# A modulation step moved one projection unit later, with other fetch places, in a fused hybrid attention layer

## What is computed

```python
mod = einsum('bd,de->be', silu(c), w_ada) + b_ada
shift, scale, gate = split(mod, 3, axis=-1)
h = rmsnorm(x, ln_gain) * (1 + scale[:, None]) + shift[:, None]
proj = einsum('btd,de->bte', h, w_in)
q_a, ckv, krope, g_a, q_b, k_b, v_b, q_i, k_i, w_i, g_b = split(proj, ...)
...   # latent attention (group A), sparse top-k attention (group B)
y = concat([rmsnorm(o_a, out_gain_a) * silu(g_a), rmsnorm(o_b, out_gain_b) * silu(g_b)])
out = x + gate[:, None] * (y @ w_out)      # and a last rmsnorm
```

## Time and profile before

| | us |
|---|---|
| median of three runs | 912.44 |
| lowest and highest of them | 912.41, 913.57 |
| the profiled execution | 913.76 |
| its span, from first to last instruction | 912.0 |
| TensorE busy in the span | 882.1 (97%) |
| VectorE, ScalarE busy | 414.2 (45%), 322.9 (35%) |

### The profile page before, as it was taken

One profiled execution on the slowest core, in us unless ns is written; L12 is line 12 of the kernel. 1 busy time (PEld: TensorE's weight loads), 2 busy tenths in 40 slices (PEclk: granted clock), 3 DMA queues, 4 the chain that ended last, 5 costly groups with the idle time before them and its releaser, 6 DMA issues.

```text
span 912.0 us, 13675 instructions
## 1 busy us (share of the span) xinstructions
PE 882.1 (97%) x5533; PEld 767.9 (84%) x5533; DVE 414.2 (45%) x851; ACT 322.9 (35%) x600; POOL 119.2 (13%) x191
## 2 busy tenths in 40 slices
PE   3899999999999999999999999999999999999996
PEld 1376788999999688888999998999999999888886
DVE  3522443335422144443333268464455566677362
ACT  3222343433421243322322254332334345554252
POOL 1000003101200000102120301000122223530000
PEclk9899999999999999999999999999999999999999
DMA  8999956475443222557553377755698843793413
GB/s 341 408 408 409 406 200 222 149 258 175 142 125 111 71 91 86 164 156 243 166 160 107 117 247 255 268 186 180 232 322 282 263 146 110 274 300 122 136 57 129
DMA packets 53599, 187.43 MB, mean 206 GB/s; under 512 B 7872, under 2 KB 8568, under 8 KB 52384
## 3 DMA queue, kind: packets, MB, share of 16 engines
q1 hardware_dynamic: 39488, 141.32, 43.7%
q0 software_dynamic: 13904, 44.71, 15.4%
q10 hardware_dynamic: 144, 0.52, 0.1%
HBM read 175.93 MB, written 12.69 MB: 207 GB/s over the span
## 4 chain that ended last, share of the span: by engine, by line
PE 84%; DVE 3%; ACT 2%; issue 1%; ACTq 0%; DVEq 0%
PE proj L1821 34%; PE proj L1810 28%; PE proj L1840 2%; PE proj L1791 2%; PE bankO L1919 2%; PE bankO L1928 2%; PE bankS L1840 1%; PE bankS L1982 1%; DVE w_lo L1302 1%; PE bankO L2001 1%; PE bankO L2000 1%; PE bankO L2009 1%; PE bankO L1969 1%; PE bankS L1810 1%; PE bankS L2025 1%
## 5 line engine op out<-in xcount | busy, mean ns | idle before, releaser
L1302 DVE TENSOR_TENSOR w_lo<-raw,w_hi 128x1024 fp32r<-128x1024 f32 (+2 forms) x164 | 196.8, 1205 | 227.5 <-ACT w_hi L979 226.6
L979 ACT ACTIVATE w_hi<-raw 128x1024 fp32r<-128x1024 f32 (+2 forms) x164 | 167.6, 1026 | 204.5 <-PE proj L1810 102.7
L1821 PE MATMUL proj<-hT_hi,w_hi 128*128 128x384 f32 x608 | 210.9, 347 | 0.0
L1821 PE MATMUL proj<-hT_hi,w_lo 128*128 128x384 f32 x608 | 203.8, 335 | 0.0
L1821 PE MATMUL proj<-hT_lo,w_hi 128*128 128x384 f32 x608 | 203.4, 335 | 0.0
L1810 PE MATMUL proj<-w_hi,hT_hi 128*128 128x512 f32 (+2 forms) x464 | 178.8, 385 | 1.8 <-DVE w_lo L1302 1.5
L1810 PE MATMUL proj<-w_hi,hT_lo 128*128 128x512 f32 (+2 forms) x464 | 174.3, 376 | 0.0
L1810 PE MATMUL proj<-w_lo,hT_hi 128*128 128x512 f32 (+2 forms) x464 | 174.1, 375 | 0.0
L1821 PEld LDWEIGHTS proj<-hT_hi,w_hi 128*128 128x128 f32 x608 | 114.2, 188 | 9.5 <-issue 7.8
L1821 PEld LDWEIGHTS proj<-hT_lo,w_hi 128*128 128x128 f32 x608 | 114.3, 188 | 0.5 <-issue 0.2
L1821 PEld LDWEIGHTS proj<-hT_hi,w_lo 128*128 128x128 f32 x608 | 114.1, 188 | 0.0
(11 more groups left out here) (372 smaller groups left out, 1044.3 us busy)
## 6 DMA issues: line engine op xcount, KB each, us to landing
raw<-in_units SPq DMA_DIRECT2D x184, 512.0 KB, 3.8
araw<-in_units SPq DMA_DIRECT2D x64, 512.0 KB, 8.8
kcT<-in_dsa_k_t POOLq DMA_DIRECT2D x8, 512.0 KB, 6.5
vc<-in_cache_dsa_v POOLq DMA_DIRECT2D x8, 512.0 KB, 5.8
gate_scratch<-stage POOLq DMA_DIRECT2D x8, 384.0 KB, 3.4
raw<-in_units SPq DMA_DIRECT2D x8, 336.0 KB, 4.4
raw<-in_units SPq DMA_DIRECT2D x8, 320.0 KB, 5.1
x_sb<-in_x_prompt SPq DMA_DIRECT2D x2, 1024.0 KB, 6.6
```

Source lines behind the costliest of these rows:

```text
L979: return nc.scalar.activation(out, in_, func, scale=scale, **kw)
L1302: V.tensor_tensor(w_lo[:, SLOT[u], 0:w], raw_of(u)[:, 0:w], high(u)[:, 0:w].bitcast(F32), ALU.subtract).then_inc(lo_ready, 1)
L1821: ins = mm(banks[blk][:, 0:TOK], w[:, n, cols], a[:, kt, :], start=first and n == m == 0, stop=final and n == per - 1 and m == 2)
```

## The change

The order of a quarter becomes: four ada units, a kb0 unit, five ada, a ga0 unit, seven ada, a ga1 unit, then `modT`, then a kb0 unit. The steps `modT`, `h` and `hl` of quarters 1 to 3 are put at the ga1 unit, one unit after the quarter's last ada unit. The projection units are fetched 4, 3, 2 or 0 places ahead instead of 6. From the ga1 unit of quarters 1 and 2 on, one unit more is split than LEAD would give. VectorE's step `rk` waits for the store of ga1 instead of ga0. Steps that are placed from the end of ada3 (`ld_const`, `bias` and others) come one unit earlier, since ada3 now ends one unit earlier.

```diff
-        out += ada[:4] + [keys[2 * q - 2]] + ada[4:8] + [first[q - 1]] + ada[8:12] + [keys[2 * q - 1]] + ada[12:]
-        out.append(second[q - 1])
+        out += ada[:4] + [keys[2 * q - 2]] + ada[4:9] + [first[q - 1]] + ada[9:] + [second[q - 1], keys[2 * q - 1]]
...
-AHEAD = 6
+AHEAD = {(CHUNK_OF["kb", 0], 2 * q): 4 for q in range(4)}
+AHEAD.update({(CHUNK_OF["ga", 1], q): 2 for q in range(4)})
+AHEAD.update({(CHUNK_OF["kb", 0], 2 * q + 1): 0 for q in range(4)})
...
-    for u in [u for u in order if CHUNKS[UNITS[u][0]][0] != "ada" and u < last + 3]:
+    for u in [u for u in order if CHUNKS[UNITS[u][0]][0] != "ada" and u < last + 2]:
...
-        order.insert(max(first, at - AHEAD), u)
+        order.insert(max(first, at - AHEAD.get(UNITS[u], LEAD)), u)
...
     if u < FIRST_UNIT["ckv", 0]:
-        return near
+        turns = [LAST_UNIT["ada", q] + 1 for q in (1, 2)]
+        return max([near] + [sum(v <= w + 6 for v in SPLIT_UNITS) for w in turns if w <= u])
...
-        u = LAST_UNIT["ada", q]
+        u = LAST_UNIT["ada", q] + (q > 0)
...
-            stored(dve, "ga", 0)
+            stored(dve, "ga", 1)
```

More of the change, by code:

```diff
@@ L156, in halved @@
         return 0
-    near = sum(v <= u + LEAD for v in SPLIT_UNITS)
+    done, near = sum(v <= u for v in SPLIT_UNITS), sum(v <= u + LEAD for v in SPLIT_UNITS)
     if u < FIRST_UNIT["ckv", 0]:
-        return near
-    return min(max(near, sum(v <= u for v in SPLIT_UNITS) + LEAD - 1), SPLIT_OF[W3_UNITS[LEAD - 1]])
+        turns = [LAST_UNIT["ada", q] + 1 for q in (1, 2)]
+        return max([near] + [sum(v <= w + 6 for v in SPLIT_UNITS) for w in turns if w <= u])
+    return min(max(near, done + LEAD - 1), SPLIT_OF[W3_UNITS[LEAD - 1]])
 def splits(u):
```

## The result

| | before | after |
|---|---|---|
| median of 19 runs each, us | 913.05 | 914.60 |
| lowest and highest | 912.37, 914.52 | 913.14, 916.91 |
| ratio of after to before, 95% interval | | 1.0015 (1.0009 to 1.0021) |
| the profiled execution | 913.76 | 913.14 |
| its span | 912.0 | 911.4 |

The changed kernel is slower by 1.5 us. I had forecast 911.2 us, faster by 1.2 us. The two profiled executions point the other way round, and this has to be known before one reads them: the profile of before is an execution above its median, and the profile of after is the fastest of its 19. A second profile of after is among the experiments.

The account below looks back on a forecast made before the run. DMA and TensorE were taken as both full. Idle of 2.98 us leaves and 2.9 comes; 0.2 us of the first block and about 0.35 a quarter remain: 1.25 us gained, put on the median, 911.2 us, range 909.9 to 912.4.

Parts of the forecast that it names:

- The ring: Ada buffers in quarters 1 to 3: fetches get 4.0 to 4.2 us to land; no gap taken, 3.8 us at 5.4 each.
- Rival 3: Ada buffers run dry in quarters 1 to 3, delaying place 77 by 3.8 us: 915.0 us, slower; chance 0.12.
- rival 4: Granted clock falls at a quarter's end; one fall in quarter 3 costs 5.1 us: 916.3 us; chance 0.08.
- The median: Whole kernel: the 1.25 us shift, 912.5 us for the profiled execution, was put on the median of before: 911.2 us.
- Rival 2: No gain: the new order ends on a landing, whatever time the clock lost before it: 912.4 us; chance 0.15.
- The cadence: Fetched units up to place 77 land every 1.283 us without a break, kb0.7 near 114.2 us.
- The removed waits: TensorE's waits for `modA` (quarters 1 to 3) and for `w_lo` at kb0.2 and kb0.4 go: 2.98 us.
- the new ones: TensorE waits 0.5, 0.8, 0.8 us before ada1.15, ada2.15, ada3.15 and 0.8 us for `hT_lo` at kb0.6: 2.9 us.
- The split of kb0.7 ahead of `modT`: End of quarter 3: its `w_lo` delays VectorE, so TensorE waits 0.8 us for `hT_lo`; kb0.6 starts at 120.4 us.
- No dip of the clock: Sign: the forecast is wrong if the granted clock dips after 50 us.
- The term for fewer ada groups: Each quarter gains about 0.35 us: one ada group fewer to switch to, and tails of matmuls before the waits.
- rival 1: New waits don't form since units land earlier than expected: 4.2 us gained, 908.2 us; chance 0.10.

Follow-up runs that it names:

- twelve buffers: The changed kernel with twelve instead of eight buffers for ada units, in use from quarter 1 on: 912.54 us, ratio 0.9992.
- before, ring of 12: The kernel before with twelve instead of eight ada buffers, orders as before: 913.51 us, ratio 1.0002.
- the same, last split late: The changed kernel with twelve ada buffers, and kb0.7 split behind the modulation of quarter 3 instead of ahead of it: 911.64 us, ratio 0.9983.
- before with the early splits: The kernel before, with kb0.2 and kb0.4 split before the modulation of quarters 1 and 2, order unchanged: 912.47 us, ratio 0.9991.
- before, ring of 6: The kernel before with six instead of eight ada buffers, all orders as before: 915.34 us, ratio 1.0028.
- after without the early splits: The changed kernel with kb0.2 and kb0.4 split behind the modulation again: 915.69 us.
- after, old fetch places: The changed kernel with every projection unit fetched 6 places ahead again, eight ada buffers: 918.56 us, ratio 1.0054.
- The halved ada units: Both kernels with half of each ada unit not fetched, the first half multiplied twice (wrong results): old order 911.99 us, new order 908.80 us.

## Why the prediction was wrong

The forecast of 911.2 us missed by 3.4 us, and the runs split this in two.

**The ring, 2.1 us: the failed step.** The prediction said: "I take no gap, since the nearer row is the unsaturated one: a fetch that would leave a gap meets an idle queue." With twelve buffers, where the gap does not arise, the same order takes 912.54 us, not 914.60. The trace counts sixteen arrivals for each fetch, and I read each as one of the sixteen DMA engines being through with its share (the times are worked out from the trace; no view lists them, and they don't name the engine). In the first trace of after:

| | issued | first arrival | last arrival |
|---|---|---|---|
| ada1.11 | 42.17 | 50.55 | 52.71 |
| ada1.12 | 49.58 | 52.68 | 53.98 |

By this reading the engines are 2.2 us apart. When ada1.12 is issued the fastest has 1.0 us of work left, and its next share arrives 3.1 us after the issue: 2.13 us from arrival to arrival instead of 1.28, 0.85 lost. The slowest has 3.1 us left and loses nothing. So the rate falls to 260 GB/s and the landing at 53.98 is still in time. What is lost is the lead of the fast engines: the distance shrinks from 2.2 to 1.3 us. A later delay of single engines, which that lead would have hidden, now makes the unit late. In the first trace of after kb0.2 (place 36) lands 0.36 us late in that way; in the second a unit at place 60 lands 1.3 us late, its other arrivals within 0.2 us of their time. In the trace of after with twelve buffers the engines stay 2.4 us apart from place 25 to the end, and no unit is late, though three arrivals at place 38 are 0.3 to 0.5 us late. At kb0.7 the first arrival is at 112.26 us before and 112.04 with twelve buffers, and at 113.50 and 114.14 in the two traces of after: there the fast engines have lost 1.5 and 2.1 us. Such delays of single engines stand in all traces; what makes them was not tried.

I had priced the ring as if one fetch landed late at each quarter and the queue were whole again after it. The shortest fetch of `araw` after 45 us sorts the traces:

| kernel | shortest, us | kb0.7 landed, us | median, us |
|---|---|---|---|
| before, ring of 12 | 12.6 | 113.97 | 913.51 |
| after, ring of 12 | 10.4 | 114.42 | 912.54 |
| the same, last split late | 10.4 | 113.92 | 911.64 |
| before with the early splits | 6.5 | 113.96 | 912.47 |
| before, two traces | 5.4, 6.6 | 114.18, 114.29 | 913.05 |
| after, two traces | 4.4, 4.2 | 114.97, 116.54 | 914.60 |
| before, ring of 6 | 4.0 | 116.68 | 915.34 |
| after without the early splits | 3.7 | 118.19 | 915.69 |
| after, old fetch places | 3.3 | 120.18 | 918.56 |

From 5.4 us on the last landing lies within 0.5 us of 114.2; at 4.4 and less it is late, and the later the shorter (of the 116.54 us in the second trace of after, 1.3 are the single engine). I had the bound of 5.4 us in the earlier trace rows, the only row of the saturated stretch, and took the 3.8 us of the earlier trace rows instead, a median over the whole kernel. Rival 3 had the right mechanism, and it got 0.12. That its 915.0 us is close to 914.60 is luck: its delay of 3.8 us measured 2.1, and the 911.2 us that it is added to measured 912.54. Two of the sums around it were slightly off: the gain is eaten from 4.55 us on (0.55 + 0.35 + 0.35 = 1.25) and not from 4.8, and rival 4 with the half of rival 3 makes 0.14 and not 0.15.

**The median, 1.3 us.** From the layout I had 912.5 us for the profiled execution, and then wrote "I put the shift on the median", 911.2 us. That median was of three executions, 912.44; of 19 it is 913.05, which is 0.6 of the 1.3 us. Rival 2 contradicts that step in the same text: the new order ends on a landing, whatever happened before. The order with twelve buffers bears rival 2 out: 912.54 us, with kb0.6 at 120.46, and hardly any spread. A shift read in one execution may be put on the median only if the time lost before it, here at the clock, is still lost in the new order.

**What held.** The cadence: kb0.7 lands between 113.96 and 114.42 us in every trace with a shortest fetch of 5.4 us or more (forecast 114.2). The removed waits, the new ones and their places. The split of kb0.7 ahead of `modT` in quarter 3: its wait was 0.52 us, forecast 0.8, and removing its cause, with twelve buffers, gained 0.9 us in the median. No dip of the clock between 50 and 900 us in the two traces of after.

**The term for fewer ada groups was right, and its counterpart was left out.** I gave each quarter 0.35 us for one ada group fewer and for tails of matmuls before the removed waits. The halved ada units show it without a wait for DMA. kb0.2 and kb0.4 start there, in the old order and in the new one, at:

```profile
68.52 0.50 PE L1810 MATMUL proj<-w_hi,hT_hi 128*128 128x512 f32 x1 [0.76 <-DVE w_lo L1302]
...
94.92 0.50 PE L1810 MATMUL proj<-w_hi,hT_hi 128*128 128x512 f32 x1 [0.73 <-DVE w_lo L1302]
```

```profile
68.33 0.50 PE L1812 MATMUL proj<-w_hi,hT_hi 128*128 128x512 f32 x1
...
93.03 0.50 PE L1812 MATMUL proj<-w_hi,hT_hi 128*128 128x512 f32 x1
```

The old order takes 26.40 us, less waits of 0.50 and 0.73 that is 25.17; the new one takes 24.70 (forecast 24.8). In after the same stretch is 96.21 - 70.27 = 25.94 us, less two waits for `araw` of 0.17 and 0.65 that is 25.12, and before it is 26.39 - 1.23 = 25.16 us. With twelve buffers there is one wait, of 0.64 us, and the rest is 24.92. So each new wait costs some 0.2 us beside its idle time, a tail of matmuls of its own: the eight matmuls before a wait last 0.64 us in the timeline, and eight in an unbroken group take 0.47 (four units in 1.87 us). I had counted the tails that go and not those that come, and in after they cancel. In quarter 3 (kb0.4 to kb0.6) the halved units gain nothing beyond the waits. That, and a wait of 0.39 us for `w_lo` that came, go towards explaining why they gained 3.2 us in the median where rival 1 had 4.2.

**What stays open.** Why one execution of after takes 913.1 and another 916.9 us is explained only in part, by single engines that are late at different places. In the second trace the rate also falls from 80 to 82 us, after an issue of SyncE that took 1.16 us where most take 0.43 (issues of 1.3 and 1.4 us stand in the first trace too); I did not find out why. Three of the 19 runs (916.5 to 916.9) have a mean granted clock of 0.988 against 0.990 to 0.995 in the others; a dip, as with the old fetch places, would fit, but no trace of such a run exists.

## What to carry to other kernels

Where a ring of buffers feeds a full DMA queue, an order that makes the consumer use its units in longer bursts needs a deeper ring: look for the fetch with the least time from its buffer's release to its use, and compare that with the shortest fetch seen in the same saturated stretch, not with a median. A wait on the consumer is not always hidden by a later landing, since it also frees buffers later. When a change makes a stage end on a landing, its time is the landing's time, not the old median less the saved waits.

## What the hardware showed

A landing is the slowest of sixteen arrivals, and in the two traces of after these lie 1.1 to 2.6 us apart over the whole stretch. So DMA can lose rate (260 GB/s for 2 us) with no unit late, and a unit can be late (1.3 us at place 60) with the rate at 404 to 406 around it. The Trainium skill, "DMA: Bandwidth & Descriptors", section Why a DMA increments its semaphore by 16 and not by 1, says that the engines of a transfer finish independently and that only the full count means a landing. The trace agrees, with the 2.2 us of ada1.11.

TensorE's granted clock fell after waits of 1.9 and 1.7 us with the old fetch places (0.55 from 60.3 to 64 us), and it did not fall after the wait of 1.6 us in the second trace of after, where it reads 1.00 from 52 to 76 us. The Trainium skill, "TensorE: Matmul & The Clock Gate", section HAM oscillation, describes matmul groups that end in DMA waits and begin again at half clock. The kernel with the old fetch places agrees for its first such wait (0.55 right behind it); after the second, which ended at 88.66 us, the clock fell only at 91 us.
